# Projections of the short convolution moved between the steps of the banded attention, with another map of SBUF

## What is computed

```python
proj = x @ w_in[l]
(q_lat, kv_lat, k_rope, sc_b, sc_c, sc_h, cf_a, cf_g, gq_q, gq_k, gq_v) = jnp.split(proj, split_points, axis=-1)
y_a = mla_attention(q_lat, kv_lat, k_rope, ...)            # 4 heads, dense, 16 blocks of 128 queries
y_b = sc_b * depthwise_conv(sc_c * sc_h, sconv_w[l])       # 3 taps, 256 channels
y_c = conformer_conv(cf_a, cf_g, cconv_w[l], ...)          # GLU, 31 taps, LayerNorm, swish
y_d = window_gqa(gq_q, gq_k, gq_v, sink[l], ...)           # 4 heads, |i-j| <= 128, 4 blocks of 128 queries
mix = jnp.concatenate([y_a, y_b, y_c, y_d], axis=-1) @ w_out[l]
x = layer_norm(DEEPNORM_ALPHA * x + mix, ln1_g[l], ln1_b[l])
x = layer_norm(DEEPNORM_ALPHA * x + expert_choice_moe(x, ...), ln2_g[l], ln2_b[l])   # 16 experts, 64 tokens each
```

## Time and profile before

| | |
|---|---|
| median of 3 runs | 1618.19 us (1615.17 to 1618.88) |
| the profiled execution, its time | 1619.66 us |
| its span in the trace | 1617.9 us |
| TensorE busy | 1377.7 us, 85% |
| VectorE, ScalarE, GpSimd busy | 32%, 18%, 14% |
| HBM read | 451.18 MB |

### The profile page before, as it was taken

The page is one execution under the profiler, slowest core; times in us unless marked ns, Lnnn a source line. Parts: engine busy times, 40 slices in busy tenths (PEclk is TensorE's granted clock), DMA queues, the critical chain, the costliest instruction groups (busy, mean ns, idle before and its releaser), DMA issues.

```text
span 1617.9 us, 14766 instructions
## 1 busy us (share of the span) xinstructions
PE 1377.7 (85%) x5984; PEld 688.0 (43%) x5984; DVE 519.4 (32%) x937; ACT 298.9 (18%) x523; POOL 231.6 (14%) x162
## 2 busy tenths in 40 slices
PE   5998789479999888889679978992999999889893
PEld 4874358433333323333268734682333333233231
DVE  4574863601101101110439367445011111101105
ACT  3234560100000000000132255401000000000000
POOL 2443500000000000000234444011000000000003
PEclk9999599689999999999899975995999999999997
DMA  9411001789999999999680200108999999999992
GB/s 347 161 52 52 1 6 74 303 324 427 427 427 428 426 430 427 427 427 428 238 329 2 104 0 1 53 40 344 376 427 427 428 428 426 428 427 428 428 427 82
DMA packets 42482, 462.62 MB, mean 286 GB/s; under 512 B 6704, under 2 KB 7344, under 8 KB 14000
## 3 DMA queue, kind: packets, MB, share of 16 engines
q1 hardware_dynamic: 31968, 432.62, 63.7%
q0 software_dynamic: 4032, 14.68, 2.5%
q10 hardware_dynamic: 6416, 14.39, 2.4%
HBM read 451.18 MB, written 10.49 MB: 285 GB/s over the span
## 4 chain that ended last, share of the span: by engine, by line
PE 62%; DMA 19%; DVE 8%; issue 4%; ACT 2%; POOL 2%; POOLq 1%; DVEq 0%; ACTq 0%; SPq 0%
DMA ring<-w_moe 19%; PE bank L750 17%; PE bank L447 11%; PE bank L773 10%; PE bank L728 7%; PE bank L595 2%; PE bank L692 2%; PE bank L694 2%; PE bank L693 2%; PE bank L411 1%; DVE stat L1001 1%; PE bank L524 1%; PE bank L583 1%; PE bank L635 1%; POOLq L358 1%
## 5 line engine op out<-in xcount | busy, mean ns | idle before, releaser
L750 PE MATMUL bank<-ring,work 128*64 128x512 f32 x2048 | 451.2, 597 | 34.0 <-DMA ring<-w_moe 22.2
L750 PEld LDWEIGHTS bank<-ring,work 128*64 128x64 f32 x2048 | 166.3, 138 | 308.9 <-issue 251.2
L773 PE MATMUL bank<-ring,work 128*64 128x512 f32 x1024 | 231.2, 597 | 28.1 <-DMA ring<-w_moe 16.3
L1176 DVE TENSOR_TENSOR X<-X,bank 128x512 f32<-128x512 f32 x128 | 88.0, 687 | 314.1 <-PE bank L728 313.9
L1164 DVE TENSOR_TENSOR work<-work,bank 128x512 f32<-128x512 f32 x32 | 22.0, 688 | 500.3 <-PE bank L750 498.5
L773 PEld LDWEIGHTS bank<-ring,work 128*64 128x64 f32 x1024 | 77.0, 137 | 170.0 <-issue 143.1
L728 PE MATMUL bank<-work 128*128 128x512 f32 x256 | 125.6, 620 | 13.1 <-ACT work L1427 11.1
L1416 ACT ACTIVATE work<-bank 128x512 f32<-128x512 f32 x64 | 38.2, 597 | 357.9 <-PE bank L411 357.9
L1540 POOL COPY cur<-slot_i 128x1 int32<-128x1 int32 x16 | 2.9, 184 | 610.6 <-PE bank L411 553.5
L1477 POOL TENSOR_TENSOR w_lo<-ring,w_hi 128x2048 fp32r<-128x2048 f32 x16 | 73.6, 4601 | 111.6 <-ACT w_hi L1225 79.4
L447 PE MATMUL bank<-x_hi,w_hi 128*128 128x512 f32 x288 | 77.2, 413 | 13.3 <-POOL w_lo L1477 7.7
(11 more groups left out here) (194 smaller groups left out, 1379.6 us busy)
## 6 DMA issues: line engine op xcount, KB each, us to landing
ring<-w_moe SPq DMA_DIRECT2D x192, 2048.0 KB, 29.2
ring<-w_in SPq DMA_DIRECT2D x18, 1024.0 KB, 13.0
ring<-w_out SPq DMA_DIRECT2D x8, 1024.0 KB, 22.7
out<-X POOLq DMA_DIRECT2D x12, 512.0 KB, 8.3
X<-out ACTq DMA_DIRECT2D x2, 2048.0 KB, 8.5
x_rows<-X ACTq DMA_DIRECT2D x8, 512.0 KB, 2.8
X<-x_in ACTq DMA_DIRECT2D x4, 512.0 KB, 7.9
ring<-ln SPq DMA_DIRECT2D x2, 1024.0 KB, 6.7
```

The lines of the kernel that those rows point to most:

```text
L750: ins = mm(B((kind, pair, n))[64 * e:64 * e + 64, :], xsT[:, k, 64 * e:64 * e + 64], w[:, e, n * 512:(n + 1) * 512], start=(k == 0), stop= ...
L773: ins = mm(B(("O", pair, n))[64 * e:64 * e + 64, :], hidT[:, k, 64 * e:64 * e + 64], w[:, i, e], start=(k == 0), stop=(k == KD - 1))
L1176: nc.vector.tensor_tensor(X[:, t, cols], X[:, t, cols], B(name)[:, :], ALU.add)\
```

## The change

- Projections 12 to 17 are now the short convolution's. Latents, keys, queries, values and `KROPE` take numbers 4 to 11.
- D is made in rounds of a whole block: four maxima, then one pair of small operations for all four heads, four exponentials, one sum and one reciprocal, four scalings. Between the transposes and scores of rounds 0 to 2 stand the three passes of two projections each.
- VectorE takes the latents' scalings and three rotation products (`kv_scaled`, `d_sines`, `q_scaled`) between the taps of the long convolution, and the short convolution in round 2. Of D's 16 row-sums only 4 remain.
- GpSimd's low parts of chunks 7 and 8 stand inside D, and the splits of `mix` and of `w_out` behind them, most after the last round.
- P, its transpose, Q, K and later x1T lie in the freed ring slots 0 to 3; `x_lo` is reused as the high part of `mix`; the table `TURN` says which slots the pieces take. The `ln1` vectors no longer take a slot.
- A layer's nine chunks of `w_in` and three of `w_out` are each allowed by the last piece that used their slot, not by the new x's transposes.
- The first `mix` product no longer waits for the read-out of the last attention output (its `logits` bank is another one), and piece 2 is allowed at that product.

The core of the diff:

```diff
-CF_G, CF_A, SC_C, SC_H, SC_B, KV, GQK, QLAT, GQQ, GQV, KROPE = 0, 2, 4, 6, 8, 10, 11, 12, 14, 16, 17
+CF_G, CF_A, KV, GQK, QLAT, GQQ, GQV, KROPE, SC_C, SC_H, SC_B = 0, 2, 4, 5, 6, 8, 10, 11, 12, 14, 16
...
+X_HI_SLOT, W_HI_SLOT = 12, 14
+OUT_RAW = (8, 9, 10, 11)
+OUT_HI = (13, 5, 4, 12)
+P_SLOT, PT_SLOT, Q_SLOT, K_SLOT = 0, 1, 2, 3
...
+TURN = (6, 14, 0, 4, 8, 10, 12, 2)
+TURNS = len(TURN)
...
+def ring_loads():
+    order = [("w", n) for n in range(IN_SLOTS)] + [("wout", j) for j in (2, 1, 3)]
+    order += [("piece", 0), ("wout", 0), ("piece", 1), ("piece", 2)]
+    order += [("piece", m) for m in range(3, PIECES)]
...
+def freed_before(kind, n):
+    if kind == "w":
+        slot = n
+    elif kind == "wout":
+        slot = OUT_RAW[n]
+    else:
+        slot = TURN[n % TURNS]
+        if n >= TURNS:
+            return 0, FREED["chunk", JOINED * (n - TURNS) + JOINED - 1]
+        return 0, FREED[{6: ("w", 7), 14: ("w", 8), 0: "attention", 2: "logits"}.get(slot, "mix")]
+    if (kind, n) == ("wout", 0):
+        return 0, FREED["w", 8]
+    last = PIECES - TURNS + TURN.index(slot - slot % 2)
+    return -1, FREED["chunk", JOINED * last + JOINED - 1]
...
-                for i in range(NT * GQ_H):
-                    n, h = divmod(i, GQ_H)
-                    lo, hi = window(n)
-                    if i + 3 < NT * GQ_H:
-                        d_scores(i + 3)
-                    pe.wait_ge(dp_ready, at(lay, NT * GQ_H, i + 1))
...
-                    if i + 4 == NT * GQ_H:
-                        pe.wait_ge(keys_ready, at(lay, 1, 1))
-                        pe.wait_ge(queries_ready, at(lay, MLA_H, MLA_H))
...
+                for n in range(NT - 1):
+                    first, second = SC_C + 2 * n, SC_C + 2 * n + 1
+                    d_turned(n, 0)
+                    d_scores(n + 1, 0)
+                    project(first, HI_HI)
+                    d_turned(n, 1)
+                    d_scores(n + 1, 1)
+                    project(first, HI_LO)
+                    d_turned(n, 2)
+                    d_scores(n + 1, 2)
+                    project(first, LO_HI)
+                    if n == 0:
+                        read_out(pe, ("gvT",), lay)
+                    d_values(n, 0)
+                    d_turned(n, 3)
+                    d_scores(n + 1, 3)
+                    if n == 0:
+                        q_rotated()
+                    project(second, HI_HI)
+                    project(second, HI_LO)
+                    d_values(n, 1)
+                    project(second, LO_HI)
+                pe.wait_ge(keys_ready, at(lay, 1, 1))
+                pe.wait_ge(queries_ready, at(lay, MLA_H, MLA_H))
+                for j in range(MLA_H // 2):
+                    read_out(pe, ("kup", j), lay)
+                a_scores(0)
+                a_scores(1)
+                n = NT - 1
+                d_turned(n, 0, retire=1)
+                a_scores(2)
+                d_turned(n, 1)
+                a_scores(3)
+                d_turned(n, 2)
+                d_turned(n, 3)
...
                 for tap in range(1, CF_K):
+                    if tap == 11:
+                        kv_scaled()
+                    if tap == 14:
+                        d_sines(0)
+                    if tap == 23:
+                        q_scaled()
+                    if tap == 28:
+                        d_sines(1)
...
+                def d_max(n):
                     off, w = d_width(n)
-                    if i >= GQ_H:
-                        full(v, ("TD", i - GQ_H), lay)
+                    own = slice(GQ_H * n, GQ_H * n + GQ_H)
+                    for h in range(GQ_H):
+                        i = GQ_H * n + h
+                        if n > 0:
+                            full(v, ("TD", i - GQ_H), lay)
+                            v.sem_inc(passed["dve"], 1)
+                        full(v, ("SD", i), lay)
                         v.sem_inc(passed["dve"], 1)
-                    full(v, ("SD", i), lay)
-                    v.sem_inc(passed["dve"], 1)
-                    ins = nc.vector.tensor_tensor_reduce(p_d[:, h, 0:w], B(("SD", i))[:, 0:w], band[:, off:off + w],
-                                                         1.0, -3.0e38, ALU.add, ALU.max, mx[:, i:i + 1])
-                    ins.then_inc(freesem(("SD", i)), 1)
-                    read_out(v, ("SD", i), lay)
-                    c = PAR["sink"] + h
-                    nc.vector.tensor_scalar(nmx[:, i:i + 1], mx[:, i:i + 1], par[:, c:c + 1], -1.0,
-                                            ALU.max, ALU.mult).then_inc(dmax_ready, 1)
-                def d_norm(i):
-                    n, h = divmod(i, GQ_H)
+                        nc.vector.tensor_tensor_reduce(p_d[:, h, 0:w], B(("SD", i))[:, 0:w], band[:, off:off + w],
+                                                       1.0, -3.0e38, ALU.add, ALU.max, mx[:, i:i + 1])\
...
+                k_sine()
                 d_max(0)
+                cf_centred()
+                k_rope()
+                d_norm(0)
                 d_max(1)
-                for i in range(NT * GQ_H):
-                    if i + 2 < NT * GQ_H:
-                        d_max(i + 2)
-                    else:
-                        a_max(i + 2 - NT * GQ_H)
-                    d_norm(i)
-                    if i == 1:
-                        k_rope()
-                    elif i % 2 == 1 and i <= 2 * MLA_H + 1:
-                        q_rope(i // 2 - 1)
+                q_sines()
+                cf_scaled()
+                d_norm(1)
+                d_max(2)
+                q_rope()
+                short_conv()
+                cf_gated()
+                d_norm(2)
+                d_max(3)
+                a_max(0)
+                a_max(1)
+                d_norm(3)
+                a_max(2)
...
+                for n in range(1, 5):
                     w_low(n)
+                d_rope(0)
+                w_low(5)
+                w_low(6)
+                d_rope(1)
+                d_rope(2)
+                r = slice(NOPE, QK)
+                hold(rope_d_ready, at(lay, 3, 3))
+                hold(fullsem(("rotK",)), bank_count(("rotK",), lay, 1)[1])
+                tt(Kh[r, 0, :], Kh[r, 0, :], cos_a[r, :], ALU.mult).then_inc(cos_a_done, 1)
+                hold(cos_a_done, at(lay, 3, 1))
+                w_low(7)
+                hold(w_lo_ready, at(lay, IN_SLOTS - 1, 7))
+                hold(rope_k_ready, at(lay, 1, 1))
+                for h in range(1, MLA_H):
+                    ins = nc.gpsimd.tensor_copy(Kh[r, h, :], Kh[r, 0, :])
+                ins.then_inc(keys_ready, 1)
+                hold(keys_ready, at(lay, 1, 1))
+                hold(fullsem(("rotQ",)), bank_count(("rotQ",), lay, 1)[1])
+                for h in range(0, MLA_H, 2):
+                    tt(Qh[r, h:h + 2, :], Qh[r, h:h + 2, :], cos_a[r, :].unsqueeze(1).broadcast_to([ROPE, 2, S]),
+                       ALU.mult).then_inc(cos_a_done, 1)
+                hold(cos_a_done, at(lay, 3, 3))
+                w_low(8)
                 for j in range(2):
                     hold(freesem(("in", SC_C + j)), bank_count(("in", SC_C + j), lay, 2)[1])
...
-                hold(keys_ready, at(lay, 1, 1))
+                wout_lower(1)
+                hold(freed, at(lay, N_FREED, FREED["w", IN_SLOTS - 1]))
                 hold(yc_ready, at(lay, 2, 2))
-                for k in MIX_ORDER[0:4]:
-                    nc.gpsimd.tensor_copy(mix_hi[:, k], mix[:, k]).then_inc(split_hi, 1)
-                for n in range(4):
-                    j = MIX_ORDER[2 * n] // 2
-                    hold(wout_hi_ready, at(lay, 4, n + 1))
-                    tt(wout_low[j], ring[:, (WOUT_AT + j) % RING], wout_hi[j].bitcast(F32), ALU.subtract)\
-                        .then_inc(wout_lo_ready, 1)
-                    if n < 2:
-                        hold(split_hi, at(lay, 4, 4))
-                        for k in MIX_ORDER[2 * n:2 * n + 2]:
-                            tt(mix_lo[:, k], mix[:, k], mix_hi[:, k].bitcast(F32), ALU.subtract)\
-                                .then_inc(split_ready, 1)
+                mix_split(0)
+                hold(yb_ready, at(lay, 2, 2))
+                mix_split(1)
+                wout_lower(2)
+                hold(freesem(("YD", NT - 1)), bank_count(("YD", NT - 1), lay, 2)[1])
+                mix_split(2)
+                wout_lower(3)
                 for t in range(NT):
```

More of the change, by code:

```diff
@@ L458, in _ @@
                 for i in range(2):
[L459 to L460 removed]
+                    project(i, HI_HI)
                 for t in range(NT):
@@ L476, in _, with turned_by, summed @@
+                def turned_by(name, rows):
+                    before(pe, name, lay)
+                    mm(B(name)[:, :], rot_d, rows, start=True, stop=True).then_inc(fullsem(name), 1)
+                def summed(name, parts):
+                    before(pe, name, lay)
+                    for n, part in enumerate(parts):
```

(23 more changed lines are left out.)

711 lines of the change are left out of this document (357 added, 354 removed).

## The result

| | before | after |
|---|---|---|
| median | 1618.54 us (1615.17 to 1619.55) | 1645.67 us (1641.34 to 1647.82, 4 runs) |
| ratio, 95% interval | 1 | 1.0168 (1.0150 to 1.0185) |
| profiled execution, span | 1619.7, 1617.9 us | 1641.34, 1639.5 us |

The change makes the kernel **27 us slower**. The forecast was 1606 us in a range of 1583 to 1621, with 0.18 for slower: the size, the sign and the range are wrong.

The account below looks back on a forecast made before the run. The weights (DMA) bound the experts, so gains ahead come off in full: 1.5 us in layer 0, 6.1 in layer 1, 4.3 between, together 11.9 off 1619.7, giving 1607.8 profiled and 1606 us median, range 1583 to 1621.

Parts of the forecast that it names:

- What bounds the kernel, and the experts: Experts: bound by the weights' DMA, their length stays, and what a layer gains ahead comes off in full.
- Piece 2 and `ln1` load with x's return: Start of `mix`: these loads cost nothing, covered by 17 us of TensorE work; up to 2 us without that cover.
- P to mix, 204.7 us: From the start of projection 2 to the first `mix` product: 204.7 us, where before it took 204.0 and 210.8.
- half a hold of 4.5: Round 2, up to the last `d_norm`: VectorE waits half of a 4.5 us GpSimd instruction, within 25.2 us.
- Layer 1: ... 6.1: Layer 1, projection 2 to `mix`: 210.8 us fall to 204.7, 6.1 gained.
- Rival D: D and A: every first comer blocks the other engine fully, 8 us per layer more, 1622 us; chance 0.10.
- Rival A: Ahead of `mix`: holds and clock cost little, 11 us per layer fall away, 1584 us; chance 0.25.
- Rival B: Banded attention: the clock stays down, one round of three in each layer runs slow, 1628 us; chance 0.13.
- C: Banded attention and border: no gain, holes as long as before, stores and drain don't couple, 1618 us; chance 0.07.
- Between the layers, 4.3 us: Weight chunks allowed sooner, so GpSimd's drain behind x's stores ends earlier: 4.3 us gained, bounds 0 and 6.4.
- The serial piece: End of round 1: `d_norm(2)` stands on VectorE behind the short convolution, and TensorE idles 12.2 us.

Follow-up runs that it names:

- experiment 4: e4_start_piece with x's return as four loads, one a tile, and VectorE waiting for each where used: 1620.35 us, ratio 1.0017.
- experiment 2: Two runs on the changed kernel, e2_piece (piece 2 after x's return) and e3_ln1 (`ln1` after it): 1629.27 and 1636.84 us.
- experiment 1: The changed kernel, with layer 0's first weight load waiting until x_in has landed: 1637.61 us, ratio 1.0107.
- experiment 7: The kernel before the change, with layer 0's nine weight loads not waiting, so beside x_in: 1626.60 us, ratio 1.0057.
- e1 to e5: Changed kernel with first weight load after x_in; piece 2 after x's return; `ln1` after it; first two; these plus four-tile return: 1637.61, 1629.27, 1636.84, 1622.19, 1620.35 us.
- experiments 8 and 9: 8: block 3's scaling ahead of latent maxima, on e6_conv_later, 1590.77 us; 9: each low part of `w_out` in four instructions, on e4_start_piece, 1605.28 us.
- quarters alone: e4_start_piece with each GpSimd low part of `w_out` cut from one instruction into four: 1605.28 us, ratio 0.9930.
- e4_start_piece: The changed kernel, with layer 0's first weight load waiting for x_in and piece 2 for x's return: 1622.19 us, ratio 1.0025.
- experiment 6: e4_start_piece, with layer 1's weight loads 4 to 8 and those of `w_out` waiting for the transposes, as before the change: 1631.54 us, ratio 1.0072.
- experiment 5: e4_start_piece, with the short convolution and the long one's gating moved behind the scaling of block 2 on VectorE: 1600.56 us, ratio 0.9896.
- e2_piece: The changed kernel, with piece 2 (2 MB) waiting until x has come back: 1629.27 us, ratio 1.0057.
- e3_ln1: The changed kernel, with `ln1` (1 MB) loaded only once x has come back: 1636.84 us, ratio 1.0114.
- e6_conv_later: The kernel of experiment 5: e4_start_piece with short convolution and gating behind the scaling of block 2: 1600.56 us, ratio 0.9896.

## Why the prediction was wrong

*What bounds the kernel, and the experts.* Right: they last as long as before (461.4 us for 461.6), and what was lost or gained ahead of them showed in the time.

*"Piece 2 and `ln1` load with x's return ... it would cost up to 2 us without."* **This is the step that failed most.** It took the 17 us until TensorE turns the first tile for cover, and asked neither how long the return would take with 3 MB beside it nor what VectorE has to do between the two. The cover ends some 10.6 us into `mix`, since the additions and the norm need 6.0 (experiment 4). For the return the numbers were there: alone, 2.1 MB landed after 8.5 us, 3.5 more than 2.1 / 0.42; 5.2 MB make 12.5 + 3.5 = 16.0. It measured 16.6, and cost 9.3 and 9.0 us of the trace. Piece 2 alone is 7 us a layer (experiment 2).

*The start of layer 0.* **A failed step by omission**: the prediction has no term for it. Before, TensorE gave the slots free for the weight loads, and only after it had waited for x; so a wait for a free slot also kept the order of two transfers (the first weight load went out at 12.04, now at 1.64). The new bookkeeping finds layer 0's slots free and waits for nothing. 8 us (experiment 1), and 9 the other way round (experiment 7). For the parameters I had looked at which loads stand ahead in the queue; the same look at x_in was missing.

*P to mix, 204.7 us.* The path was right to the round: 108.1 us to the first transposes of round 0's end (forecast 107.4), then 30.6 (31.3), one idle of 11.8 (forecast 12.2) behind the convolution. Mis-sized: *"half a hold of 4.5"* ahead of the last `d_norm`, which was a whole one, 28.1 for 25.2; and 41.3 for 40.8 after it, of which A took 33.8. In layer 1 it was 214.7. Over six kernels whose order is the same (changed, e1 to e5) the twelve stretches are 208.1 to 215.9 us, 212.4 in the mean: 7.7 over the forecast. So of *"Layer 1: ... 6.1"* nothing came.

*Rivals.* Rival D (0.10) said "every first comer blocks fully", 8 us a layer more: 212.7, near the mean just named. The runs bear its mechanism out: beside a GpSimd instruction of 4.5 us a scaling of VectorE takes 4.55 or 4.01 us, where alone it takes under 0.5 (experiments 8 and 9). The Trainium skill's rule (SBUF — State Buffer, "Who interferes with whom"), that the other engine "fully blocks", agrees with these rows, and deserved more than a tenth. That its 8 us fit so well is in part luck: in layer 0 of the changed kernel only 3.4 us were missing, and the mean has the clock's differences in it too. Rival A, that holds cost little (the holds it lists make 12.8 us, with its 2 taken off the 11 that it uses), is out: quarters alone gave 10 to 12 us per layer in the traces, 15 us in all by the ratios. Rival B is out in its form: a round runs at full clock; but after the idle of 11.8 us a pass took 3.78 us. C's time, 1618, lies near that of e4_start_piece, but not by its mechanism: round 1 ran without a hole.

*Between the layers, 4.3 us.* More was gained, 6.6 us to P, but for the most part by another way. The drain was to end 4.3 us sooner (827.2 less 822.6 is 4.6, and the 1.5 us for the landing stand on no row) and to last 9 to 10 us. It lasted 11.9 for 13.8, a step of 1.9 us at most, since drains of 12.1 and 12.3 came with late loads as well (experiment 6). The rest came since the wait for the low part now stands behind two passes, which the prediction did not have: luck.

*The serial piece.* Booked as a fixed cost of the change, 12 us a layer. Its size was right (11.8 for 12.2). But it was a choice of order, and undoing it the largest single gain (experiment 5).

## What to carry to other kernels

When a change frees buffers earlier, list for each load what it now runs beside, and divide the sum of the bytes by the DMA rate, and add what a lone transfer takes beyond that (3.5 us here): a small transfer that a queue of engines waits for must not share with one that nobody needs yet. A wait on a buffer may also be the only thing that orders two transfers; look for what a removed wait did besides. When a transfer is to hide under TensorE's work, subtract from the cover what another engine has to do between its landing and TensorE's next step. And where GpSimd and VectorE run together, cut GpSimd's long instructions and issue the scalings that TensorE waits for ahead of everything that doesn't hurry.

## What the runs showed of the hardware

- Transfers under way together slowed each other by their size: 2 MB landed after 8.5, 11.9, 13.9 and 16.6 us with 0, 1, 2 and 3 MB beside them (before, e2_piece, e3_ln1, the changed kernel).
- A scaling on VectorE that takes 0.49 us alone took 4.01 behind the start of a GpSimd instruction of 4.5 us, and 1.55 when that was cut in four. Four scalings in a row took 1.14 us alone, 5.34 beside one GpSimd instruction and 5.13 beside four short ones.
- Four instructions of 512 columns on GpSimd took 5.1 to 5.5 us, once 6.8, where one of 2048 took 4.5, once 5.1, and yet the program gained 0.95%.
- In round 1 of e6_conv_later a pass took 3.68 us right after a round with idles under 1.4 us, and P to the first transposes of block 1 ran from 105.6 to 112.1 us in kernels with the same order there. With the same order of instructions the clock does not fall at the same points in every trace, and a trace apart by 4 us in this stretch proves nothing.
